# A transformer-like block on one core: the last gated embedding by row halves, its last product in two banks, and post norms by column half

## The reference, cut to what matters

```
h = h + rms_norm(merged @ w_out, norm_mix_post)              # product "wo", post norm 1
f = conv_ffn(rms_norm(h, norm_ffn_pre), ...)                 # its last product is "dn"
h = h + rms_norm(f, norm_ffn_post)                           # post norm 2
...                                                          # state space layer, embedding 0
h = h + (o * silu(gate)) @ attn_out_w                        # product "ao", sums ("fo", i, f)
g = sigmoid(rms_norm_2(h, ple_norm_w[1]) @ ple_gate_w[1])    # 1024 x 1024, "pg1"
return h + g * (p[1] @ ple_proj_w[1])                        # "pp1"; this is the output
```

## Time and profile before

| | us |
|---|---|
| three runs | 965.90, 968.73, 972.37 |
| median | 968.73 |
| the profiled execution's own time | 967.78 |
| its span in the profile | 965.9 |
| PE busy | 918.3 (95%) |
| PE weight loads busy | 805.4 (83%) |
| DVE busy | 682.6 (71%) |
| ACT busy | 523.3 (54%) |
| mean share of full clock granted to PE | 0.985 |

### The profile page before, as it was taken

How to read it: one execution, slowest core, us unless ns; L and a number is a source line. 1 busy time by engine, 2 the same in 40 slices (tenths; PEclk the granted TensorE clock), 3 DMA queues, 4 the chain that set the end, 5 groups by cost and what they waited for, 6 DMA issues and landing times.

```text
span 965.9 us, 14423 instructions
## 1 busy us (share of the span) xinstructions
PE 918.3 (95%) x5697; PEld 805.4 (83%) x5697; DVE 682.6 (71%) x969; ACT 523.3 (54%) x783; POOL 64.2 (7%) x67
## 2 busy tenths in 40 slices
PE   6999999999999979999999799899899998999977
PEld 6988998988888769999988799878787876878756
DVE  6688727965867588888843878784676777866544
ACT  6862332333545466665634667756666485467433
POOL 5002422410000000000000000000000000000000
PEclk9999999999999989999999899999999999999989
DMA  9542132122555546565555346543223453621231
GB/s 309 163 167 89 44 115 88 44 88 88 194 177 175 174 131 208 185 197 196 182 205 180 106 147 190 168 138 130 89 88 124 159 197 110 208 98 44 89 130 44
DMA packets 80835, 136.63 MB, mean 141 GB/s; under 512 B 3941, under 2 KB 46273, under 8 KB 80768
## 3 DMA queue, kind: packets, MB, share of 16 engines
q1 hardware_dynamic: 78656, 131.17, 41.0%
q0 software_dynamic: 2112, 4.53, 1.5%
HBM read 134.64 MB, written 1.05 MB: 140 GB/s over the span
## 4 chain that ended last, share of the span: by engine, by line
PE 62%; ACT 7%; DVE 6%; issue 4%; DMA 1%; DVEq 0%; ACTq 0%
PE bank L432 17%; PE bank L434 17%; PE bank L433 17%; PE bank L421 3%; ACT upper L1228 2%; DVE lower L1763 2%; PE bank L1067 1%; PE bank L869 1%; PE bank L1051 1%; ACT arena L1693 1%; PE bank L679 1%; PE bank L878 1%; DMA loaded<-in_ffn_w_up 1%; DVE h L1844 1%; ACT arena L1320 0%
## 5 line engine op out<-in xcount | busy, mean ns | idle before, releaser
L1763 DVE TENSOR_TENSOR lower<-loaded,upper 128x2048 fp32r<-128x2048 f32 x122 | 277.9, 2283 | 124.3 <-ACT upper L1228 121.9
L1228 ACT ACTIVATE upper<-loaded 128x2048 fp32r<-128x2048 f32 x122 | 231.9, 1903 | 110.3 <-PE bank L434 98.9
L432 PE MATMUL bank<-xT_upper,upper 128*128 128x256 f32 (+1 forms) x664 | 188.2, 283 | 1.7 <-DVE xT_lower L1828 1.7
L433 PE MATMUL bank<-xT_lower,upper 128*128 128x256 f32 (+1 forms) x664 | 186.5, 281 | 0.0
L434 PE MATMUL bank<-xT_upper,lower 128*128 128x256 f32 (+1 forms) x664 | 186.3, 281 | 0.0
L432 PE MATMUL bank<-upper,xT_upper 128*128 128x512 f32 x352 | 147.1, 418 | 8.1 <-DVE lower L1763 5.3
L434 PE MATMUL bank<-upper,xT_lower 128*128 128x512 f32 x352 | 139.7, 397 | 0.0
L433 PE MATMUL bank<-lower,xT_upper 128*128 128x512 f32 x352 | 139.1, 395 | 0.0
L432 PEld LDWEIGHTS bank<-xT_upper,upper 128*128 128x128 f32 (+1 forms) x664 | 126.7, 191 | 3.0 <-issue 2.9
L434 PEld LDWEIGHTS bank<-xT_upper,lower 128*128 128x128 f32 (+1 forms) x664 | 126.8, 191 | 0.1
L433 PEld LDWEIGHTS bank<-xT_lower,upper 128*128 128x128 f32 (+1 forms) x664 | 126.6, 191 | 0.1
(11 more groups left out here) (337 smaller groups left out, 1208.8 us busy)
## 6 DMA issues: line engine op xcount, KB each, us to landing
loaded<-in_w_in SPq DMA_DIRECT2D x26, 1024.0 KB, 5.2
loaded<-in_ffn_w_up SPq DMA_DIRECT2D x22, 1024.0 KB, 5.2
loaded<-in_ssm_in_w SPq DMA_DIRECT2D x20, 1024.0 KB, 5.2
loaded<-in_ffn_w_down SPq DMA_DIRECT2D x11, 1024.0 KB, 5.0
loaded<-in_ssm_out_w SPq DMA_DIRECT2D x8, 1024.0 KB, 5.0
loaded<-in_ple_gate_w SPq DMA_DIRECT2D x8, 1024.0 KB, 5.1
loaded<-in_attn_in_w SPq DMA_DIRECT2D x8, 1024.0 KB, 5.2
loaded<-in_w_branch_ret SPq DMA_DIRECT2D x4, 1024.0 KB, 5.0
```

The source lines that it names most:

```text
L432: mm(out, a[0], b[0], start=start, stop=False)
L433: mm(out, a[0], b[1], start=False, stop=False)
L1228: A(part(upper, PARTS, n), part(loaded, LOADS, n), ACT.Copy).then_inc(uppers, 1)
L1763: TT(part(lower, LOADS, n), part(loaded, LOADS, n), part(upper, PARTS, n).bitcast(F32), sub) \
```

## The change

There are four parts.

1. `deep_product`: in the tail, the column halves are separated. For each row tile, first all tail tiles of f = 0, then all of f = 1. A piece of `before` stands ahead of the f = 0 step. A unit is counted as used when all 8 of its (tile, i, f) steps are done.
2. Post norms: ACT no longer waits for DVE between its two squares. DVE goes f = 0, then f = 1, each after ACT has squared that bank.
3. The end: `embed(1)` is written out anew. On PE, `norm_turns(5, (0,))` stands between the 6th and the 7th `ao_tile` of row tile 1. Then come the gate pieces (f, inner half, i) in the order (0,0,0), (0,1,0), `norm_turns(5, (1,))`, (1,0,0), (0,0,1), (0,1,1), (1,0,1), (1,1,0), (1,1,1). ACT and DVE get an order to match, with the square root's table loaded ahead of `upper_of(aoT, ("aoT", 1, 1), 4, 1)`, and with the weight conversions placed between the norm's steps. The norm's row tile 1 uses banks 1 and 3.
4. The last sum (f = 1, i = 1) is made in two banks of 256 columns, bank 3 for the first and bank 0 for the second, so that there are five sigmoids, products, sums and output transfers (`LAST`).

```diff
+            elif n == 5:
+                banks = (1, 3) if i else (0, 1)
...
+        LAST = [(0, 0, 0, slice(0, 512)), (0, 1, 1, slice(0, 512)), (1, 0, 0, slice(0, 512)),
+                (1, 1, 1, slice(0, 256)), (1, 1, 2, slice(256, 512))]
...
-                order = ([(t, i) for i in range(2) for t in range(lead)] +
-                         [(t, i) for t in range(lead, n - tail) for i in range(2)] +
-                         [(t, i) for i in range(2) for t in range(n - tail, n)])
-                ps, ws, left = {}, {}, [4] * (n // 2)
+                order = ([(t, i, (0, 1)) for i in range(2) for t in range(lead)] +
+                         [(t, i, (0, 1)) for t in range(lead, n - tail) for i in range(2)] +
+                         [(t, i, (f,)) for i in range(2) for f in range(2) for t in range(n - tail, n)])
+                ps, ws, left = {}, {}, [8] * (n // 2)
...
-            for t in range(4, 8):
-                ao_tile(t, 1)
+            ao_tile(4, 1)
+            ao_tile(5, 1)
+            norm_turns(5, (0,))
+            ao_tile(6, 1)
+            ao_tile(7, 1)
             embedding_product(1, 1, 1)
-            embed(1)
+            gate_piece(0, 0, 0, 0)
+            gate_piece(0, 1, 0, 0)
+            norm_turns(5, (1,))
+            gate_piece(1, 0, 0, 2)
+            used("pg10.0", gate_piece(0, 0, 1, 1))
+            gate_piece(0, 1, 1, 1)
+            used("pg10.1", key=("pg", 1, 0, 1))
+            gate_piece(1, 0, 1, 3, slice(0, 256))
+            used("pg11.0", gate_piece(1, 0, 1, 0, slice(256, 512), ("pg", 1, 1, 2)))
+            gate_piece(1, 1, 0, 2)
+            gate_piece(1, 1, 1, 3, slice(0, 256))
+            gate_piece(1, 1, 1, 0, slice(256, 512), ("pg", 1, 1, 2))
+            used("pg11.1", key=("pg", 1, 1, 2))
...
-                act.wait_ge(sem("post_weighed"), 4 * (n - 1) + z + 1)
...
+            root_table()
             upper_of(aoT, ("aoT", 1, 1), 4, 1)
-            embed(1)
+            row_sums(5, 0)
+            split_to("ao3", 1)
+            norm_upper(5, xT, (0,))
+            split_to("ao3", 2)
+            row_sums(5, 1)
+            split_to("pg10.1")
+            norm_upper(5, xT, (1,))
+            for f, i, p, c in LAST:
+                z = 2 * f + i
+                ps = full(act, ("pg", 1, f, p))
+                act.wait_ge(sem("ple_used"), 3 + z)
+                empty(A(psg[:, z % 2, c], ps[:, c], ACT.Sigmoid), ("pg", 1, f, p))
+                if z == 0:
+                    split_to("pg10.1", 1)
...
-                for f in (1, 0):
-                    if f == 0:
-                        ve.wait_ge(sem("post_sq"), 4 * (m - 1) + 2 * i + 1)
+                for f in range(2):
+                    ve.wait_ge(sem("post_sq"), 4 * (m - 1) + 2 * i + f + 1)
...
-            embed(1)
+            row_scale(5, 0)
+            scale(5, 0, xT, "ple_norm_w_2", 8)
+            split_to("ao3", 1)
+            lower_rows(5, 0, xT)
+            plain_join("fo", 1)
+            split_to("ao3", 2)
+            row_scale(5, 1)
+            split_to("pg10.1")
+            scale(5, 1, xT, "ple_norm_w_2", 8)
+            lower_rows(5, 1, xT)
+            for f, i, p, c in LAST:
...
+                ins = TT(tmph[:, i, d], psg[:, z % 2, c], ps[:, c], mul)
+                ins.then_inc(sem("ple_used"), 1)
+                ve.wait_ge(sem("ple_used"), 5 + z + (p == 2))
+                TT(h[:, i, d], h[:, i, d], tmph[:, i, d], add).then_inc(sem("out_ready"), 1)
+                if z == 0:
+                    split_to("pg10.1", 1)
```

More of the change, by code:

```diff
@@ L389, in pieces @@
         def pieces(n, i):
[L391 removed]
+            if n == 3:
                 banks = (2 * i, 2 * i + 1)
+            elif n == 5:
+                banks = (1, 3) if i else (0, 1)
             elif n == 4:
@@ L488, in deep_product @@
             def deep_product(name, n, xt, key, banks, before={}, lead=0, tail=0):
-                order = ([(t, i) for i in range(2) for t in range(lead)] +
-                         [(t, i) for t in range(lead, n - tail) for i in range(2)] +
-                         [(t, i) for i in range(2) for t in range(n - tail, n)])
-                ps, ws, left = {}, {}, [4] * (n // 2)
-                for t, i in order:
-                    if (t, i) in before:
+                order = ([(t, i, (0, 1)) for i in range(2) for t in range(lead)] +
+                         [(t, i, (0, 1)) for t in range(lead, n - tail) for i in range(2)] +
+                         [(t, i, (f,)) for i in range(2) for f in range(2) for t in range(n - tail, n)])
+                ps, ws, left = {}, {}, [8] * (n // 2)
+                for t, i, fs in order:
+                    if (t, i) in before and fs[0] == 0:
                         before[t, i]()
@@ L500, in deep_product @@
                         ws[u] = unit(f"{name}{u}")
-                    for f in range(2):
+                    for f in fs:
                         if t == 0:
@@ L507, in deep_product @@
                             fill(last, (key, i, f))
-                    left[u] -= 1
+                    left[u] -= len(fs)
                     if left[u] == 0:
@@ L990, in embed @@
                     rows_by_tile(f"pg{m}{f}", [("pg", m, f, i) for i in range(2)], (2 * f, 2 * f + 1), xT,
-                                 lambda blocks: xT_ready(n, blocks), (lambda: norm_turns(n, (1,))) if m and f == 0 else None)
+                                 lambda blocks: xT_ready(n, blocks), None)
             embed(0)
@@ L1105, in _, with gate_piece @@
             embedding_product(1, 1, 0)
-            for t in range(4, 8):
-                ao_tile(t, 1)
-            embedding_product(1, 1, 1)
-            embed(1)
+            ao_tile(4, 1)
[3 more added lines that the diff above has]
+            ao_tile(7, 1)
+            embedding_product(1, 1, 1)
+            def gate_piece(f, half, i, bank, c=slice(0, 512), key=None):
+                key = key or ("pg", 1, f, i)
+                w = unit(f"pg1{f}.{half}")
+                if half == 0:
+                    take(pe, key, bank)
+                for k in range(4):
+                    xT_ready(5, 8 * i + 4 * half + k + 1)
+                    last = mm3(PS[bank][:, c], both(xT, every, 4 * half + k, slice(i * P, i * P + P)),
+                               both(w, every, k, c), half + k == 0, half == 1 and k == 3)
+                if half:
+                    fill(last, key)
+                return last
+            gate_piece(0, 0, 0, 0)
[11 more added lines that the diff above has]
+            used("pg11.1", key=("pg", 1, 1, 2))
         @block.sync
@@ L1135, in _ @@
             out_rows = out.rearrange("o (i p) d -> p (o i) d", p=P)
-            for z in range(4):
-                c = slice(512 * (z // 2), 512 * (z // 2) + 512)
+            for z, (f, i, part_, c) in enumerate(LAST):
+                c = slice(512 * f + c.start, 512 * f + c.stop)
                 sp.wait_ge(sem("out_ready"), z + 1)
-                sp.dma_start(out_rows[:, z % 2, c], h[:, z % 2, c]).then_inc(sem("out_written"), 16)
-            sp.wait_ge(sem("out_written"), 64)
+                sp.dma_start(out_rows[:, i, c], h[:, i, c]).then_inc(sem("out_written"), 16)
+            sp.wait_ge(sem("out_written"), 16 * len(LAST))
         @block.gpsimd
@@ L2611, in _ @@
             lower_of(aoT, ("aoT", 1, 1), 4, 1)
-            embed(1)
+            row_scale(5, 0)
[9 more added lines that the diff above has]
+            for f, i, p, c in LAST:
+                z = 2 * f + i
+                d = slice(512 * f + c.start, 512 * f + c.stop)
+                emptied(ve, ("pg", 1, f, p))
+                ps = full(ve, ("pp", 1, f, i))
+                ins = TT(tmph[:, i, d], psg[:, z % 2, c], ps[:, c], mul)
[4 more added lines that the diff above has]
+                    split_to("pg10.1", 1)
 def kernel(**inputs):
```

1 line of the change is left out of this document (removed).

## The result

The changed kernel took 958.01 us (median of four runs, 955.35 to 959.5) against 967.92 us for the kernel before (four runs). The ratio is 0.9884, 95% interval 0.9852 to 0.9916: faster by 0.8 to 1.5%. The profiled execution took 959.5 us, with a span of 957.7.

A forecast was written before the change was run, and what follows sets the result against it. PE, busy 95% of the span, was taken as the bound, through its idle and half-pace times. End 10.55 plus middle 1.6 minus half pace 1.65 saves 10.5 us: 958.2 against 968.73, range 953.8 to 963.5.

The forecast's parts named there:

- The walk through the end: Last stage: queues stepped forward with the old trace's durations in the new order; span ends at 955.35, 10.55 us less.
- the new wait: Gate product at the end: PE idles 1.65 us before the 13th gate matmul, until DVE's conversion of pg10.1 ends.
- the last steps: After PE's last matmul: 256-column sigmoid, product and sum, then 2.4 us to the span's end; 0.9 us shorter.
- Does the new 1.65 us bring half pace back?: Gate product behind the new wait: assumes one stretch of matmuls at half pace, costing 1.65 us.
- no half pace at the end: Rival, gate product: the 1.65 us wait is too short to matter; saving 12.15, 956.6 us; chance 0.27.
- The middle: Deep-product tails and post norms before the last stage: 0.4 + 0.5 + 0.7 = 1.6 us saved (0 to 3).
- The tails: Deep products: earlier merging of row tile 1's bank in `bret` saves 0.4 us; nothing in `wo`, wait 0.3 at most.
- The post norm behind `dn`: Post norm after the down product: ACT's removed wait and an earlier complete bank save 0.7 us in row tile 1.
- The one behind `wo`: Post norm after the output product: banks already complete before ACT comes to them; 0.5 us saved.
- the middle gives nothing: Rival, middle: half-pace restart eats the post norms' saving, later releases the tails'; saving 8.9, 959.8 us; chance 0.14.
- No weight load landed late: Rival, end: pg11.0 lands late and PE waits 3.5 us more; saving 7.0, 961.7 us; chance 0.17.
- The clock did not stay low: Rival, end: clock down at about 931 stays at 0.50 to the end, +16.8 us; 973.4 us; chance 0.03.

The follow-up runs named there:

- the two later series: The changed kernel, unaltered, timed twice more beside the experiments: 955.4 us (ratio 0.9859) and 954.62 us (0.9851).
- one_bank: Changed kernel with the last sum in one bank of 512 columns again, with one output transfer for it: 960.27 us, one run.
- third_time: The changed kernel, unaltered, timed a third time beside the kernel with halved weight conversions: 954.62 us, ratio 0.9851.
- again: The changed kernel as it is, timed and profiled once more: 955.4 us, ratio 0.9859.
- end_alone: Changed kernel with the old deep_product and old post norms, so only the new end: 956.89 us, ratio 0.9879.
- no_cover_again: Second run of no_cover: changed kernel with gate piece (1,0,0) moved behind (0,1,1): 959.16 us, ratio 0.9913; first run 958.27, 0.9908.
- middle_alone: Kernel before with the new deep_product and new post norms, old end: 966.9 us, ratio 0.9985 over 12 runs.
- tails_alone: Kernel before with the new deep_product only, old post norms: 967.43 us, one run.
- post_alone: Kernel before with the new post norms only, old deep_product: 966.9 us, one run.
- late_turns: Changed kernel with row tile 0's transposes put back behind all of ao and pp: 959.86 us, ratio 0.9902.
- halved_again: Second run of halved_units: changed kernel with pg10.1 and pg11.0 each converted in two halves: 954.35 us, 0.9845; first run 954.93, 0.9872.

## Why the prediction was right

The forecast was 958.2, and 958.01 was measured; the range of 953.8 to 963.5 holds it and both later medians. That closeness is partly luck. With the sizes that the traces show, 11.1 at the end and 2.5 in the middle, the same sum gives 968.73 - 13.6 = 955.1, which is what the two later series measured (955.4 and 954.62). The first series lay some 3 us above them; 4.3 us of slower pace in its profiled execution is the only reason that a trace shows.

**The walk through the end held.** The prediction's times are on before's time axis, so I give both from the start of the first matmul of `ao_tile(4, 1)`: 918.36 there (965.91 - 47.55), 921.29 in the changed kernel's trace.

| event | predicted | measured |
|---|---|---|
| row tile 0's transposes | 2.90 | 2.91 |
| first gate matmul | 8.04 | 8.16 |
| end of the new wait | 12.49 | 12.60 |
| row tile 1's transposes | 15.24 | 15.46 |
| piece (1,0,0) | 16.29 | 16.25 |
| piece (0,0,1) | 19.04 | 19.10 |
| first 256-column matmul | 24.54 | 24.59 |
| piece (1,1,0) | 27.34 | 27.31 |
| last piece | 30.14 | 30.06 |
| last matmul ends | 33.14 | 32.95 |
| end of the span | 36.99 | 36.42 |

Every queue behaved as walked: nothing on ACT, DVE or SP that PE then needed comes out more than 0.2 us from where it was put. Only pg11.1's conversion ended 0.3 later, with PE not yet there. The new wait is 1.44 where I had 1.65. The end saves 11.13 where I had 10.55; 0.36 of the difference lies in the last steps (3.49 against 3.85): 0.25 through the shorter output transfer that one_bank shows, 0.1 because DVE's last sum follows the product after 0.04 and not after the old 0.15. The other 0.2 lie before them.

**The step that failed is "Does the new 1.65 us bring half pace back?"** I took one stretch at half pace, +1.65. There was none, in any of six executions with such a wait: the changed kernel (1.44), third_time (1.47), again (1.36), end_alone (1.29), no_cover_again (1.37) and one_bank (1.38). So the rival "no half pace at the end", which I gave 0.27, is what happened. Its 956.6 is nearer to the medians of the two later series (955.4 and 954.62) than the forecast is. The error in my reasoning was to rank waits by length alone. No_cover_again has a wait of 2.14 with full pace behind it, longer than the 1.87 of before, which did bring half pace.

Nor was that 1.87 a chance event of one execution. The same wait stands in middle_alone, tails_alone and post_alone, the other kernels with the old end, and half pace followed in all of them. PE's timeline of middle_alone:

```profile
942.38 0.51 PE L432 MATMUL bank<-upper,xT_upper 128*128 128x512 f32 x1 [1.87 <-DVE xT_lower L1812]
...
943.60 0.63 PE L433 MATMUL bank<-lower,xT_upper 128*128 128x512 f32 x1
944.02 0.63 PE L434 MATMUL bank<-upper,xT_lower 128*128 128x512 f32 x1
```

What sets these four apart from the six, and from the 2.14, is what lay ahead: in each the clock had fallen within the wait of 5.3, and had come back only 3.5 to 4.1 us before PE stopped again (in before at about 937.6, with PE stopping at 941.1). Where the wait of 5.3 is gone, no short wait at the end brought half pace. The nearest to a test is no_cover_again: its 2.14 stands at the same place as the 1.87, behind row tile 1's transposes, without the 5.3 ahead of it, and full pace follows. That is one execution, and its PE order differs too, so that the earlier fall is the cause stays argued, not shown. The Trainium skill, TensorE: Matmul & The Clock Gate, section Why this matters for your kernels, warns of idle gaps between matmul bursts only from a length on that lies between the 2.14 and the 3.84 us seen here. The waits of 1.29 to 1.47 and 2.14 without half pace and that of 3.84 with it agree; the four of 1.87 do not. By that rule the forecast would have been 956.6.

**The middle was worth more than 1.6, and less of it can be kept.** The tails gave 0.33 (0.4 expected), and nothing in `wo` (nothing expected; the delay there is 0.46 where I had 0.3 at most). The post norm behind `dn` gave 0.93 (0.7); the add to h of row tile 1 starts 1.55 behind the last matmul's end, where I had 1.7. The one behind `wo` gave 1.0 to 1.2 where I had 0.5: that term was mis-sized. The prediction gives no working for it; 0.5 is about the wait of row tile 0 alone (0.54), and row tile 1 had one too (0.92). Together 2.5. The rival "the middle gives nothing" is refuted by the trace of middle_alone, but over 12 runs only some 1.2 to 1.5 us of it arrive. The trace offers a reason, the stretches at half pace later on: two in middle_alone against one in before, 1.6 us each, more than any single term of the middle. That they explain all 12 runs is argued, not shown.

**The other rivals.** No weight load landed late (pg11.0's conversion on DVE ended at 937.37, 0.2 before PE took the unit at 937.54; there was no more room than that). The clock did not stay low. The first profiled execution saved only 8.3 us by its own time (967.78 - 959.5). It holds 4.3 us of slower pace in a stage that was not changed (last section). Third_time, whose feed-forward net ran at before's pace, took 955.5, 12.28 less than before's profiled 967.78, and the prediction's terms without the half pace give 10.55 + 1.6 = 12.15. That agreement is again partly luck: the end gives 11.12 there and the stretch from 315 us to the end's start 2.96, but third_time's matmuls stand 1.86 later than before's from 100 to 315 us, where the two kernels do not differ.

**A sum in the chances.** The prediction says that a tenth of the forecast's mass was moved to "within", but its 0.64 for faster is 0.37 + 0.27, without the move; with it, it would be 0.60.

## What to carry to other kernels

When PE waits at a hand-over between stages, look for independent matmuls that can be put between the transposes and their first use, and walk all queues from there with the trace's own durations: such a walk held to 0.2 us over 33 us, while the guess about the clock behind a wait did not. A change that moves work earlier shows its next limit as a new, shorter wait; here it was the conversion of one weight unit behind its transfer, and halving the conversion on both engines removed the wait. Where a per cent is at stake, compare traces matmul by matmul, and part by part: the spans of two executions of one and the same kernel differed by 4 us, which is more than three of the four parts are worth.

## What the runs showed of the hardware that was not expected

**Two steady paces at full clock.** In the feed-forward stage, some 1,050 matmuls of 256 columns run without a gap. Their start-to-start distance is 0.113 us in some executions and 0.118 in others, for the whole stage, which makes about 4.3 us. The same window of 10 us in three traces, with the counts of PE and of its weight loads behind the busy times. The kernel before:

```profile
400.00:410.00 10.00, 10.00 (x91) 10.00 (x90) 8.79 (x13) 6.01 (x10) 0.00 (x0) 1.00 0.66 211
```

The changed kernel, first profile:

```profile
400.00:410.00 10.00, 10.00 (x88) 10.00 (x87) 8.15 (x12) 6.98 (x10) 0.00 (x0) 1.00 0.58 193
```

The changed kernel, third_time:

```profile
400.00:410.00 10.00, 10.00 (x91) 10.00 (x90) 8.57 (x13) 6.64 (x10) 0.00 (x0) 1.00 0.64 209
```

The clock is 1.00 in all of them. The profile shows no idle time of PE or of the weight loads, so no wait for a semaphore is seen; the transfers' share is no guide either: it is 0.65 in the same window of late_turns, which has the slower pace, and 0.66 and 0.64 in the two faster ones here. The pace is one or the other from the point where the clock comes back after `wo`'s post norm, and it stays until the stage ends. The faster one was seen in before, again, third_time, end_alone, middle_alone, tails_alone, post_alone, no_cover_again and halved_again; the slower one in the changed kernel's first profile, late_turns and one_bank, and in halved_units, whose granted clock there was 0.95. As the changed kernel shows both, the code alone does not fix it. The slower one came in 4 of the 8 profiles of kernels with the new end and the new middle, and in none of the 5 others; whether the code shifts the odds, and what draws the pace, stays open. The Trainium skill, TensorE: Matmul & The Clock Gate, section Back-to-back issue gap, gives columns / 2.4 GHz + 2.5 ns for an isolated matmul; an estimate from it for 256 columns is 109 ns. Both paces here are above it, by 4 and 9 ns.

**Half pace is not decided by the length of a short wait.** The kernels' stages at about 616, 701 and 804 us, the same in all kernels, fell to half pace in some executions and not in others, with waits that were alike: 2.94 us before a stretch in middle_alone, and 2.95 before none in the kernel before. Of the 13 traces without no_cover's, 6 have the stretch at 616. Each has exactly one of the other two, 11 the one at 701 and 2 (before and tails_alone) the one at 804. PE's timeline of middle_alone:

```profile
699.83 0.47 PE L432 MATMUL bank<-upper,split_arena 128*128 128x512 f32 x1 [2.94 <-DVE arena L2343]
...
701.22 0.63 PE L434 MATMUL bank<-upper,split_arena 128*128 128x512 f32 x1
```

and of the kernel before:

```profile
700.13 0.47 PE L432 MATMUL bank<-upper,split_arena 128*128 128x512 f32 x1 [2.95 <-DVE arena L2345]
...
701.37 0.40 PE L434 MATMUL bank<-upper,split_arena 128*128 128x512 f32 x1
```

In the first the clock falls between 1 and 1.4 us after the wait has ended (701.22, 0.63 long); in the second it does not fall at all there. Much shorter waits can do it too. At 804 PE idles 0.99, transposes, idles 1.26, and runs at half pace in the kernel before:

```profile
804.14 0.61 PE L432 MATMUL bank<-upper,split_arena 128*128 128x512 f32 x1 [1.26 <-DVE split_arena L1828]
804.54 0.63 PE L433 MATMUL bank<-lower,split_arena 128*128 128x512 f32 x1
```

and, behind the same two waits, at full pace in middle_alone:

```profile
804.95 0.50 PE L432 MATMUL bank<-upper,split_arena 128*128 128x512 f32 x1 [1.26 <-DVE split_arena L1827]
805.29 0.39 PE L433 MATMUL bank<-lower,split_arena 128*128 128x512 f32 x1
```

So removing such a wait is worth its length, and the half pace behind it, 1.6 us here, only as a chance. The waits of 5.3 and 1.87 at the old end brought it in all four executions.

**A table load without anything behind it.** The square root's table took 1.28 us on ACT, and the next activation followed at once (ACT's timeline of the changed kernel):

```profile
915.46 1.28 ACT L1292 ACT_TABLE_LOAD   x1
916.75 0.20 ACT L1292 ACTIVATE small<-small 128x1 f32<-128x1 f32 x1
```

The Trainium skill, ScalarE: Activation LUTs, section What ACT_TABLE_LOAD costs, gives 1283 ns for the load and about 1380 for a drain. The first agrees; of a drain behind the load this trace shows nothing. The load itself lay in an idle time of ACT, as the prediction had it, and cost nothing at the end.
